# Half-width first products, a changed order of the early loads, and two reorderings in the attention stages of a two-block kernel

## The reference

```python
h = rms_norm(x, mix_norm_g)
proj = h @ w_in                      # 512x1024 by 1024x3080
fq, fk, fv, flog, dq, dk, dv = split(proj)
log_f = log_sigmoid(flog + b_forget) # 8 columns: the forget gates
fox = softmax(fq fk^T/8 + cumsum differences of log_f, causal) @ fv
diff = (softmax(q1 k1^T) - lam * softmax(q2 k2^T)) @ dv
x = x + concat(fox, rms(diff)) @ w_out
x = x + (silu(rms(x) @ w_gate) * (rms(x) @ w_up)) @ w_down
# second block: neighbourhood attention + convolution, gates, FFN
```

## Time and profile before

| | |
|---|---|
| median of 3 runs | 1319.79 us (1319.68 to 1319.92) |
| profiled execution | 1322.61 us, its span 1320.8 us |
| PE busy | 1302.7 us, 99% of the span |
| DVE, ACT, POOL busy | 656.3, 654.7, 668.9 us |
| granted PE clock, mean | 0.996 |

### The profile page before, as it was taken

One profiled execution on the slowest core, in us unless ns is written; L12 is line 12 of the kernel. 1 busy time (PEld: TensorE's weight loads), 2 busy tenths in 40 slices (PEclk: granted clock), 3 DMA queues, 4 the chain that ended last, 5 costly groups with the idle time before them and its releaser, 6 DMA issues.

```text
span 1320.8 us, 18761 instructions
## 1 busy us (share of the span) xinstructions
PE 1302.7 (99%) x6275; PEld 1091.7 (83%) x6275; DVE 656.3 (50%) x1232; ACT 654.7 (50%) x1048; POOL 668.9 (51%) x884
## 2 busy tenths in 40 slices
PE   9999999999999999999999999999999999999997
PEld 7898888888888888888888988888888888888886
DVE  8566586652222221111698887867455455551003
ACT  4688666754444433333447776363454444442213
POOL 7423343466555555555455365556655555555551
PEclk9999999999999999999999999999999999999999
DMA  6432332233333332333363232332333333333331
GB/s 176 112 82 72 80 110 67 65 96 113 105 99 96 95 95 88 99 89 108 87 136 110 67 97 84 107 96 80 104 99 91 96 90 95 96 98 106 108 102 65
DMA packets 200577, 127.54 MB, mean 97 GB/s; under 512 B 8602, under 2 KB 193311, under 8 KB 200383
## 3 DMA queue, kind: packets, MB, share of 16 engines
q1 hardware_dynamic: 200487, 126.65, 33.5%
q10 hardware_dynamic: 24, 0.01, 0.0%
HBM read 117.82 MB, written 2.47 MB: 91 GB/s over the span
## 4 chain that ended last, share of the span: by engine, by line
PE 89%; DVE 6%; ACT 3%; issue 2%; POOL 0%; DVEq 0%; ACTq 0%; POOLq 0%
PE PS L818 27%; PE PS L819 27%; PE PS L820 27%; DVE PS L2240 1%; PE PS L1014 1%; PE PS L999 1%; PE PS L1000 1%; PE PS L1029 1%; PE PS L1030 1%; ACT PR L1464 1%; PE PS L895 0%; ACT PR L1457 0%; DVE YT L2409 0%; DVE QA L1888 0%; DVE KB L1888 0%
## 5 line engine op out<-in xcount | busy, mean ns | idle before, releaser
L789 POOL TENSOR_TENSOR WL<-RAW,WH 128x256 fp32r<-128x256 f32 x864 | 662.4, 799 | 624.8 <-ACT WH L1294 624.6
L1294 ACT ACTIVATE WH<-RAW 128x1024 fp32r<-128x1024 f32 (+1 forms) x218 | 229.1, 1052 | 424.7 <-PE PS L820 353.2
L818 PE MATMUL PS<-XH,WH 128*128 128x512 f32 x1072 | 420.9, 393 | 1.5 <-DVE V L1851 1.5
L819 PE MATMUL PS<-XL,WH 128*128 128x512 f32 x1072 | 418.5, 390 | 0.0
L820 PE MATMUL PS<-XH,WL 128*128 128x512 f32 x1072 | 418.3, 390 | 0.0
L820 PEld LDWEIGHTS PS<-XH,WL 128*128 128x128 f32 x1072 | 201.7, 188 | 43.0
L818 PEld LDWEIGHTS PS<-XH,WH 128*128 128x128 f32 x1072 | 201.6, 188 | 42.5 <-issue 2.6
L819 PEld LDWEIGHTS PS<-XL,WH 128*128 128x128 f32 x1072 | 201.8, 188 | 40.1 <-issue 0.7
L2176 DVE TENSOR_TENSOR T<-PS,R 128x512 f32<-128x512 f32 x44 | 30.3, 691 | 164.4 <-PE PS L820 157.5
L1457 ACT ACTIVATE PR<-PR,NM 128x384 f32<-128x384 f32 (+2 forms) x88 | 49.9, 567 | 42.4 <-DVE NM L2057 42.0
L818 PE MATMUL PS<-HH,WH 128*128 128x512 f32 x176 | 68.5, 389 | 0.0
(11 more groups left out here) (349 smaller groups left out, 2071.6 us busy)
## 6 DMA issues: line engine op xcount, KB each, us to landing
RAW<-in_w_up SPq DMA_DIRECT2D x66, 512.0 KB, 3.8
RAW<-in_w_in SPq DMA_DIRECT2D x60, 512.0 KB, 3.9
RAW<-in_w_down SPq DMA_DIRECT2D x38, 512.0 KB, 3.5
RAW<-in_w_gate SPq DMA_DIRECT2D x22, 512.0 KB, 3.8
RAW<-in_w_out SPq DMA_DIRECT2D x16, 512.0 KB, 3.6
QB<-QA SPq DMA_DIRECT2D x24, 128.0 KB
KA<-KA SPq DMA_DIRECT2D x24, 128.0 KB
RAW<-in_w_down SPq DMA_DIRECT2D x8, 384.0 KB, 3.2
```

Source lines behind the costliest of these rows:

```text
L789: ins = pool.tensor_tensor(WL[:, s, cs], RAW[:, s % 2, cs], WH[:, s, cs].bitcast(F32), ALU.subtract)
L818: pe.matmul(out, ah, bh, start=start, stop=False)
L819: pe.matmul(out, ah, bl, start=False, stop=False)
L1294: act.activation(WH[:, s, 0:width], RAW[:, s % 2, 0:width], ACT.Copy).then_inc(w_hi, 1)
```

## The change

Four things are done. (1) The first two x tiles (256 tokens, "early") are split and multiplied for chunks 0 to 5 ahead of the other two; units 0 and 1 are both asked for ahead of x tiles 2 and 3; the 20 idle transposes go; the square-root table is loaded by ACT at its start. (2) On SP, unit 4 goes ahead of the 15 small loads of rpb, unit 2 ahead of the 13 small loads of vectors. (3) On DVE the low part of the gate columns WFX is made ahead of the reciprocal and of four copies, and PE waits for 5 free banks there instead of 10 tiles' count. (4) In attention, DVE's `v_lo` stands right behind PTL, and PE's outputs of the fox stage stand behind the fills in every step.

```diff
         for t in range(TC):
             sp.dma_start(XTM[:, t, :], d["x"][t * P:(t + 1) * P, :]).then_inc(x_in[t], 16)
-            if t % 2:
-                load_units(t // 2, t // 2 + 1)
+            if t == 1:
+                load_units(0, 2)
         sp.dma_start(WFR[:, :, :], ...).then_inc(wf_in, 16)
+        load_units(2, 3)
         for name, r0, k, n in vec_loads[1:]:
             ...
-        load_units(2, 3)
+        load_units(3, 4)
         sp.dma_start(BFG[:, :], d["b_forget"].partition_broadcast(P)).then_inc(consts_in, 16)
         ...
-        load_units(3, 4)
+        load_units(4, 5)
         sp.wait_ge(pool_made, 1)
         for o in range(RPR):
             sp.dma_start(RPP[8 * o:8 * o + 8, 16:16 + RPC], d["rpb_2"][:, o, :]).then_inc(rpb_in, 16)
-        load_units(4, 6)
+        load_units(5, 6)
...
+        x_tile(0, range(6))
+        warm(6)
+        x_tile(1, range(6))
         pe.wait_ge(vec_ready, 1)
         pe.wait_ge(w_hi, 1)
-        first_products(0, [0, 1])
+        first_products(0, range(4), EARLY)
         pe.wait_ge(w_hi, 2)
-        first_products(1, [0, 1])
+        first_products(1, range(4), EARLY)
+        x_tile(2, range(4))
+        x_tile(3, range(4))
+        for i in range(2):
+            first_products(i, [4, 5], EARLY)
...
-        pe.wait_ge(acc_free, TL["fox0"])
+        pe.wait_ge(acc_free, 5)
...
-                if i >= n:
+                if i >= n and kind != "fox":
                     outputs(i)
                 (fills)
-                if i < n:
+                if i < n or kind == "fox":
                     outputs(i)
...
+        act.wait_ge(dve_made, 1)
+        act.activation(LAM[:, 6:7], BT[:, :], ACT.Sqrt)
         act.wait_ge(vec_ready, 1)
+        for c in range(6):
+            act.wait_ge(early_ps, c + 1)
+            act.activation(XH[:, c, 0:2 * P], PS[:, init_bank(c), 0:2 * P], ACT.Copy,
+                           scale=vcol("mix_norm_g", c)).then_inc(early_hi, 1)
+            if c % 2 and c < 4:
+                hi_part(0, c // 2)
...
+        dve.wait_ge(wf_split, 1)
+        dve.tensor_tensor(WFX[:, :, 32:40], WFR[:, :, :], WFX[:, :, 0:8].bitcast(F32), ALU.subtract).then_inc(wf_split, 1)
         dve.wait_ge(rms_tokens, 1)
         dve.reciprocal(RT[:, :], RT[:, :]).then_inc(rstd_tokens, 1)
+        x_copy(2)
...
                                       mem["PTH"][:, k0:k1, q].bitcast(F32), ALU.subtract).then_inc(ptl_done, 1)
+                for it in values_due(kind, i):
+                    v_lo(kind, it, f["fill"])
                 for kind_, head in HEAD_STEPS[kind].get(i - 1, []):
                     head_low(kind_, head)
```

More of the change, by code:

```diff
@@ L343, in program @@
     wf_split = sem("wf_split")
+    early_ps = sem("early_ps")
+    early_hi = sem("early_hi")
+    early_lo = sem("early_lo")
+    early_copy = sem("early_copy")
     sc_ready = sem("sc_ready")
@@ L905, in _, with x_tile @@
         pe.transpose(PS[:, ACC + 1, 0:8], ROWV[0:8, 0, :], IDF[0:8, 0:8]).then_inc(vec_t, 1)
-        for t in range(TC):
+        EARLY, LATE = slice(0, 2 * P), slice(2 * P, S)
+        def x_tile(t, chunks):
             pe.wait_ge(x_in[t], 16)
-            for c in range(6):
+            for c in chunks:
                 ins = x_transpose(c, t)
-                if t == TC - 1:
+                if t == 1:
+                    ins.then_inc(early_ps, 1)
+                elif t == TC - 1:
                     ins.then_inc(part_ready, 1)
-            if t < 2:
-                warm((6, 20)[t])
@@ L916, in first_products @@
-        def first_products(i, ks):
+        def first_products(i, ks, tokens=slice(0, S)):
             for k in ks:
-                pe.wait_ge(low_done, k + 1)
+                if tokens == EARLY:
+                    pe.wait_ge(early_lo, k + 1)
+                else:
+                    pe.wait_ge(low_done, k + 1)
                 w = WH[:, i, k * P:(k + 1) * P]
-                pe.matmul(PS[:, ACC + i, :], w, XH[:, k, :], start=k == 0, stop=False)
-                pe.matmul(PS[:, ACC + i, :], w, XL[:, k, :], start=False, stop=False)
+                pe.matmul(PS[:, ACC + i, tokens], w, XH[:, k, tokens], start=k == 0 and tokens != LATE, stop=False)
+                pe.matmul(PS[:, ACC + i, tokens], w, XL[:, k, tokens], start=False, stop=False)
@@ L924, in _, with late_chunk @@
+        def late_chunk(c):
+            pe.wait_ge(acc_free, c - 5)
+            for t in range(TC):
+                ins = x_transpose(c, t)
+            ins.then_inc(part_ready, 1)
+        x_tile(0, range(6))
+        warm(6)
+        x_tile(1, range(6))
         pe.wait_ge(vec_ready, 1)
         pe.wait_ge(w_hi, 1)
-        first_products(0, [0, 1])
+        first_products(0, range(4), EARLY)
         pe.wait_ge(w_hi, 2)
-        first_products(1, [0, 1])
[L929 to L934, removed]
+        first_products(1, range(4), EARLY)
@@ L935, in _ @@
+        x_tile(2, range(4))
+        x_tile(3, range(4))
+        for i in range(2):
+            first_products(i, [4, 5], EARLY)
+        x_tile(2, [4, 5])
+        x_tile(3, [4, 5])
+        for k in range(2):
+            for i in range(2):
+                first_products(i, [k], LATE)
+        late_chunk(6)
+        late_chunk(7)
+        for k in range(2, 6):
+            for i in range(2):
+                first_products(i, [k], LATE)
+        for k in (6, 7):
             for i in range(2):
@@ L1318, in _ @@
         act.dma_start(ROWV[0:8, 0, :], d["mix_norm_g"].rearrange("(a b) -> a b", b=P)).then_inc(gain_in, 16)
[L1319 removed]
+        act.wait_ge(dve_made, 1)
+        act.activation(LAM[:, 6:7], BT[:, :], ACT.Sqrt)
         act.wait_ge(vec_ready, 1)
+        for c in range(6):
[4 more added lines that the diff above has]
+                hi_part(0, c // 2)
         for c in range(KD):
             act.wait_ge(part_ready, c + 1)
[L1323 to L1325 removed]
+            if c < 2:
+                act.wait_ge(early_copy, c + 1)
+            tokens = slice(2 * P if c < 6 else 0, S)
+            act.activation(XH[:, c, tokens], PS[:, init_bank(c), tokens], ACT.Copy,
+                           scale=vcol("mix_norm_g", c)).then_inc(act_done, 1)
         hi_part(0, 2)
@@ L1806, in _ @@
         token_squares(0)
+        dve.wait_ge(vec_ready, 1)
+        x_low_early(0)
+        x_low_early(1)
+        x_copy_early(0)
+        x_copy_early(1)
+        x_low_early(2)
+        x_low_early(3)
         token_squares(1)
-        dve.wait_ge(vec_ready, 1)
+        x_low_early(4)
+        x_low_early(5)
         x_low(0)
@@ L1811, in _ @@
         x_copy(0)
-        x_low(2)
         x_copy(1)
-        for c in range(3, KD):
+        for c in range(2, KD):
             x_low(c)
```

20 lines of the change are left out of this document (12 added, 8 removed).

## The result

The changed kernel took 1321.87 us (median of 20 executions, 1318.72 to 1323.77), the kernel before 1319.82 (20 executions, 1318.69 to 1322.15): ratio 1.0013, interval 1.0007 to 1.0019 (this is the ratio on record; that of the two medians is 1.0016). The profiled executions say something else: 1322.61 us before, 1322.26 after. Both are true, and the difference between them is half of this study.

What follows compares the result with a forecast made beforehand. PE, busy 99% of the span, was taken as the bound. Opening +2.6, fox step 17 -2.2, fox end -2.9 and na 0 gave -2.5 against the profiled execution; off the median 1317.3 us, range 1313.6 to 1321.0.

Steps and rivals of the forecast that it cites:

- The low part of a value tile in na: Na stage: DVE idles 1.2 us for ACT's high part, PE's fills cover it; 0, bounds -0.5 and +0.5.
- The two stretches of low clock: PE at half clock near 102 and 147 us behind its two longest waits; 1.5 us each, both to go.
- what step 17 gives back: Fox stage: later DVE instructions and row maximum delay the next PTL, a new PE wait; +0.5, bounds 0 and 0.8.
- The opening, PE's side and the small loads: Opening: PE starts sooner but waits for FLR behind late small loads; line 964 +1.1, low clock +1.5, together +2.6.
- The landing: Opening: rpb's small loads land 1.5 us behind their last issue, RPP at 31.4; bounds 0.8 and 3.4 us.
- Fox step 17: Fox stage: PE's wait for the value tile's low part -1.2, new PTL wait +0.5, low clock -1.5; sum -2.2.
- Fox end: Last fox outputs: twelve fills ahead shorten the wait for PTL, -1.4, and low clock goes, -1.5; sum -2.9.
- Step 17 with half of the clock's loss left: Fox stage, value tile's low part: sum if half of the clock's loss remains, given as -1.0 instead of -2.2.
- the new PTL wait: Fox stage: PE waits for its outputs behind a later row maximum; +0.5, bounds nothing and 0.8.
- The rival built on it, that the clock doesn't follow these waits: Opening and fox stage: only the waits come back, +1.1 - 0.7 - 1.4 = -1.0, 1318.8 us; chance 0.11.

Runs made afterwards that it cites:

- e6: Changed kernel with unit 4 asked for behind rpb's 15 small loads instead of ahead of them; median 0.35 us below the changed kernel's.
- f1: Changed kernel with SP's small loads in before's order: 13 of vectors ahead of unit 2, 15 of rpb ahead of unit 4; median 3.5 us below the changed kernel's.
- e3: Kernel before with a value tile's low part right behind PTL in the fox stage only; median that of before.
- f2: Kernel before with fox's value tile low part behind the heads' low parts, ahead of the outputs' ML; 0.62 us gained, 0.22 given back in the profile.
- e4: Kernel before with a value tile's low part right behind PTL in the na stage only; median +2.35 us.
- f4: Kernel before, unchanged, timed and profiled afresh for the second time; ratio 1.0007 of itself.
- the controls: Two runs of the kernel before, unchanged, each timed as if it were a change; ratios 1.0011 and 1.0007.
- e7: Changed kernel with unit 4 behind rpb's small loads and na's value tile low part where it stood before; 1318.63 us.
- f3: Changed kernel with small loads in before's order, fox's value tile low part behind the heads' and na's as before; 1315.84 us, ratio 0.9965.
- e1: Changed kernel's opening alone (parts 1 to 3), with the attention stages of before; median 1.4 us above that of before.

## Why the prediction was wrong

Three steps failed. The low part of a value tile in na was put at nothing and cost 2.3 us. The two stretches of low clock were counted whole, as -3.0, in a median of executions that have about 0.9 of them on average. And what step 17 gives back was put at 0.5 and was 1.8.

*The opening, PE's side and the small loads* (+1.1 by the wait, +1.5 by the clock; forecast +2.6): right in mechanism, too large. The products with WL began at 20.76 (20.5 forecast), unit 4 was asked for at 23.75 (23.7), RPP ran at 31.09 (31.4), line 994 at 33.50 (34.0 to 34.1), 0.4 later than before and not 1.1. PE waited there for 1.25 us, and not for the 2.1 or more from which the low clock was forecast; it came all the same. Measured +1.93 against the profiled execution. The landing was right, RPP 1.6 us behind the last issue at 29.5; mis-sized were the 15 issues, 5.29 us and not the 5.83 of the earlier trace rows, and the way from RPP to FLR, 1.68 and not 1.85. But "unit 4 stands ahead of them" was told as the whole cause. I followed what is queued behind unit 4 and not what is queued behind unit 2: its wait for unit 0's split, from 6.8 to 14.1, lies ahead of everything small. e6 and f1 showed it.

*Fox step 17* (-1.2 the wait, +0.5 the new one, -1.5 the clock; forecast -2.2): the wait fell to 0.17, as said, and PE's step there is 1.34 shorter. The give-back was mis-sized: 0.45 in the same step, where the outputs now start later behind it, and 1.33 in 20-28, in three places. They are 0.28 at outputs at 116.2, 0.69 at KB (a wait of 0.45 where there was none) and 0.36 at PTL (a wait of 0.56 for 0.23). Together that is 1.8 instead of 0.5. I had priced the delay of DVE at 0.8 and let PE's slack take some of it. e3 shows that the early place alone does it, and f2 that most of it goes when the tile stands behind the heads' low parts. The clock's part was nearly right for this profile and too large for the median.

*Fox end* (-1.4 and -1.5, forecast -2.9): -2.96 between the two profiles, -1.45 without the clock's part. Right for the profile. In the median the clock's part is smaller, as below.

*na* ("I take 0, bounds -0.5 and +0.5"; "PE has fills in plenty at that point"): the largest error, +2.3. I looked at one tile of four and asked what PE had to do, not what DVE had. I saw DVE's 1.2 us of idle time (1.25 measured) and priced it at nothing, because I took DVE for idle half of the time, from the page. In this stage it isn't: 84% busy, by the window shown with e4.

*The baseline.* The sum was made of -3.0 us of low clock that had stood in one execution. Over the profile this came true: the two stretches went, one came. But in 95 executions of before, 26 have a clock of 0.999, and f4's profile has no stretch, so there was less to be had in the median than in the profile. The prediction had the warning (the profile 2.8 us above the median) and did not act on it. With 0.9 stretches before and 1.1 after, the estimates from the mean clocks, in place of two and one, the forecast would have been 1.8 us higher.

*The sum of the errors.* Clock +1.8, na +2.3, step 17 +1.1 (+0.4 without the clock instead of -0.7), opening -0.7 and the end of the span -0.7 (-0.65 to -0.89) lead from 1317.3 to 1321.1 as an estimate. The 0.8 left to the measured 1321.87 is less than the controls read of themselves (0.9 and 1.5 us).

Two figures of the prediction don't follow from its own terms. Step 17 with half of the clock's loss left is -2.2 + 0.75 = -1.45, and not -1.0. And the bounds of the landing (+0.4 and +3.0 for +1.1) and of the new PTL wait (0 and 0.8 for 0.5) give 1316.1 to 1319.5, and not 1315.8 to 1318.8. Neither would have taken in the result.

The Trainium skill, "TensorE: Matmul & The Clock Gate", section "Why this matters for your kernels", warns only of idle gaps longer than any of these. The rival built on it, that the clock doesn't follow these waits, is not borne out: the low clock stands behind the wait of 1.5 us in four profiles of six, behind that of 2.0 in six of seven, behind the wait for FLR (1.16, 1.25, 2.23) in three of three, and never behind the wait of 1.25 at the new fox end (seven profiles). e6, e7, f1 and f3 have none of the three, and 32 of their 38 executions have a mean clock of 0.999 and the other 6 of 0.998, where of the 95 of before 26 have 0.999 and 37 less than 0.998. This case's traces show it behind shorter waits than the page would have it, but not each time, and the length alone doesn't decide: behind the 1.61 us for PR in f3 and the 1.40 in e6 the clock is 1.00. Why it falls in one execution and not in the next, and at one place and not at another, is not settled; only that it goes with these three waits is shown.

The Trainium skill, "SBUF — State Buffer", section "SBUF: two separate sides", on DVE and GpSimd taking turns: the split of unit 2 took 4.65 us in the changed kernel and 4.57 in e6, beside the same squares. It agrees with what was forecast, but no run here takes it apart.

## What to carry to other kernels

Before an instruction is moved up on an in-order engine, read when its *last* input comes: ahead of that time it can only hold back what is queued behind it, and on an engine with little slack in that stage much of the idle time is paid (2.2 of 3.9 us here), some of it 50 us later. A busy share over the whole span says nothing of that stage; take the stage's own window. Put the instruction where its input comes (f2), not as early as it may stand. The same holds of a queue of loads: a large load that has to wait for its buffer belongs behind the small ones that can go at once. And a sum made on one profiled execution needs that execution's clock stretches weighed by how often they come: profile the unchanged kernel twice more, and time it once against itself.

## What the runs showed of the hardware

A stretch of low granted clock costs 1.49 and 1.57 us here, read as the difference of two executions of one program. It comes in one execution and not in another behind waits that agree to 0.02 us, and it did not come behind a wait of 1.61 us at another place. In e1 it lasted twice as long as in the others. The last store lands after 3.1 to 3.5 us in the seven profiles in which an 8 KB packet of an instruction queue falls among its packets, and after 2.6 in the seven without. And two sets of executions of one program read 1.0011 and 1.0007 of a third, beyond the 95% interval in one case: differences of 0.1% in this kernel need a control.
